# Splitting fp32 weights into two fp32r parts: operations of 512 or of 1024 elements

## The reference

```python
h = rmsnorm(x, norm_mix_g)
q, k, v, glu, gate_a, gate_c = split(h @ w_in)             # 2048 x 9216
attn = stick_breaking(q, k, v)                             # 16 heads x 64
conv = silu(layernorm(depthwise_conv(glu_a * sigmoid(glu_b), 31 taps)))
mixed = sigmoid(gate_a) * (attn @ w_pa) + sigmoid(gate_c) * (conv @ w_pc)
x = x + mixed @ w_out
h = rmsnorm(x, norm_ffn_g)
qry = h @ w_query                                          # 8 heads x 2 x 128
top 16 of 128 x 128 experts per head by product keys; gate = softmax(scores)
x = x + sum over chosen e of gate[e] * gelu(h . expert_u[e]) * expert_v[e]
y = rmsnorm(x, norm_final_g)
```

## The kernel before

| pairs | tiles of | what DVE and ACT do in between |
|---|---|---|
| 0 to 19 | q, k, v, GLU input | norm of the input, products with gathered cache pages |
| 20 to 35 | the gates | four groups of four heads of attention; 240 taps of the convolution |
| 36 to 39 | attention branch | sigmoids of the gates, layer norm, silu |
| 40 to 43 | convolution branch | `t2`, `gates`, `mx` (hi and lo of the mixed tile) |
| 44 to 51 | output projection | residual `x`, `raw2` (hi and lo), squares |
| 52 to 59 | queries | norm, scores by sub-keys |
| 60 to 123 | expert_u (the u stage) | routing (top 16), later one-hot matrices that sum into W |
| then 2 x 128 halves | expert_v, two passes | `whl` (hi and lo of a chunk of W), W times gelu(u), gathered rows for the last 32 tokens (`gacc`) |

## Time and profile before

### The profile page before, as it was taken

How to read it: one execution, slowest core, us unless ns; L and a number is a source line. 1 busy time by engine, 2 the same in 40 slices (tenths; PEclk the granted TensorE clock), 3 DMA queues, 4 the chain that set the end, 5 groups by cost and what they waited for, 6 DMA issues and landing times.

```text
span 2321.4 us, 54702 instructions
## 1 busy us (share of the span) xinstructions
PE 2273.6 (98%) x16868; PEld 2182.1 (94%) x16868; DVE 1778.7 (77%) x3349; ACT 1307.8 (56%) x2485; POOL 281.0 (12%) x339
## 2 busy tenths in 40 slices
PE   8999999999999999999999999999999999999997
PEld 7999889999999999999999999999998888999996
DVE  7775498887766667787878888886788887777777
ACT  6445355557454344444457777775655555555564
POOL 0321100002011000000000000001611112111110
PEclk9999999999999999999999999999999999999998
DMA  6887544435555456666656555556898897777774
GB/s 215 288 289 257 193 138 155 146 129 194 182 181 201 158 166 202 203 203 205 196 184 211 187 184 186 191 189 211 283 295 295 293 304 276 247 254 248 250 259 140
DMA packets 158358, 498.38 MB, mean 215 GB/s; under 512 B 20272, under 2 KB 43192, under 8 KB 158144
## 3 DMA queue, kind: packets, MB, share of 16 engines
q1 hardware_dynamic: 136096, 425.46, 57.3%
q0 software_dynamic: 22176, 71.89, 8.1%
HBM read 472.10 MB, written 25.11 MB: 214 GB/s over the span
## 4 chain that ended last, share of the span: by engine, by line
PE 57%; DMA 3%; DVE 1%; issue 1%; ACT 1%; SPq 0%; DVEq 0%; ACTq 0%
PE ps L2015 16%; PE ps L302 10%; PE ps L305 10%; PE ps L301 10%; PE ps L2019 8%; DMA raw<-expert_v 3%; PE ps L1990 1%; ACT hi L284 0%; DMA gat<-expert_v,gidx 0%; DVE whl L1861 0%; DVE lo L289 0%; PE ps L2033 0%; SPq L1512 0%; DMA raw<-u_tiles 0%; DVE gacc L1867 0%
## 5 line engine op out<-in xcount | busy, mean ns | idle before, releaser
L289 DVE TENSOR_TENSOR lo<-raw,hi 128x512 fp32r<-128x512 f32 x1504 | 1022.7, 694 | 386.3 <-ACT hi L284 333.6
L284 ACT CAST hi<-raw 128x512 fp32r<-128x512 f32 x1504 | 922.1, 618 | 591.7 <-PE ps L305 442.6
L301 PE MATMUL ps<-h_hi,hi 128*128 128x264 f32 (+1 forms) x3200 | 822.6, 286 | 5.0 <-DVE h_lo L878 2.7
L302 PE MATMUL ps<-h_lo,hi 128*128 128x264 f32 (+1 forms) x3200 | 820.0, 286 | 0.0
L301 PEld LDWEIGHTS ps<-h_hi,hi 128*128 128x128 f32 x3200 | 602.7, 188 | 13.7 <-issue 8.6
L302 PEld LDWEIGHTS ps<-h_lo,hi 128*128 128x128 f32 x3200 | 602.7, 188 | 0.1
L2015 PE MATMUL ps<-whl,hi 128*128 128x464 f32 x2048 | 521.0, 376 | 12.8 <-DVE whl L1861 10.7
L305 PE MATMUL ps<-h_hi,lo 128*128 128x264 f32 (+1 forms) x3200 | 523.4, 285 | 3.5 <-DVE lo L289 3.5
L305 PEld LDWEIGHTS ps<-h_hi,lo 128*128 128x128 f32 x3200 | 444.4, 188 | 5.0 <-DVE lo L289 4.9
L2015 PEld LDWEIGHTS ps<-whl,hi 128*128 128x128 f32 x2048 | 349.0, 191 | 41.3 <-issue 17.0
L2019 PEld LDWEIGHTS ps<-whl,lo 128*128 128x128 f32 x2048 | 307.9, 190 | 22.6
(11 more groups left out here) (285 smaller groups left out, 1960.8 us busy)
## 6 DMA issues: line engine op xcount, KB each, us to landing
raw<-u_tiles SPq DMA_DIRECT2D x256, 512.0 KB, 3.7
raw<-expert_v SPq DMA_DIRECT2D x256, 512.0 KB, 5.4
raw<-weights SPq DMA_DIRECT2D x240, 512.0 KB, 3.5
u_spill<-ust POOLq DMA_DIRECT2D x128, 132.0 KB, 2.9
urg<-u_spill SPq DMA_DIRECT2D x32, 464.0 KB, 6.4
qb<-q_spill POOLq DMA_DIRECT2D x8, 512.0 KB, 5.8
x<-xT SPq DMA_DIRECT2D x4, 560.0 KB, 6.8
kvT<-qkv SPq DMA_DIRECT2D x1, 2240.0 KB, 12.5
```

The lines of the kernel that those rows point to most:

```text
L284: nc.scalar.copy(hi[k % SPLIT][:], raw_quarter(k)).then_inc(hi_done, 1)
L289: nc.vector.tensor_tensor(lo[k % SPLIT][:], raw_quarter(k), hi[k % SPLIT][:].bitcast(F32), ALU.subtract).then_inc(lo_done, 1)
L301: pe.matmul(out, a, rhs[0][:, first + j, 0:n], start=start and j == 0, stop=False)
L302: pe.matmul(out, a, rhs[1][:, first + j, 0:n], start=False, stop=False)
```

## The change

One ACT operation and one DVE operation now split both quarters of a half. The buffers are two halves for `hi` and two for `lo`, in the room of the four quarters; `hi[s]` and `lo[s]` become views of them, so that the matmuls read the same addresses. An operation is issued at odd k, for quarters k-1 and k, with the waits that the split of quarter k had; at even k nothing is issued. The semaphores go up by 2. All else stays as it is: PE's waits, the loads, the order and AHEAD. Since AHEAD is 3, the operations stand at the first and the third of the four positions of a tile, and in the passes over expert_v at the first of the two.

```diff
-    hi = [place(f"hi{s}", at["raw"] + 2048 * s, [P, QT, P], F32R) for s in range(SPLIT)]
-    lo = [place(f"lo{s}", at["hi3"] + 2048 * s, [P, QT, P], F32R) for s in range(SPLIT)]
-    ident = place("ident", at["lo3"], [P, P])
+    hi_half = [place(f"hi_half{s}", at["raw"] + 4096 * s, [P, HALF, P], F32R) for s in range(2)]
+    lo_half = [place(f"lo_half{s}", at["hi_half1"] + 4096 * s, [P, HALF, P], F32R) for s in range(2)]
+    hi = [hi_half[s // 2][:, QT * (s % 2):QT * (s % 2) + QT] for s in range(SPLIT)]
+    lo = [lo_half[s // 2][:, QT * (s % 2):QT * (s % 2) + QT] for s in range(SPLIT)]
+    ident = place("ident", at["lo_half1"], [P, P])
...
-    def raw_quarter(k):
-        return raw[:, k // 2 % RAW, QT * (k % 2):QT * (k % 2) + QT]
-
     def split_hi(act, q0, k):
 
-        act.wait_ge(raw_in[k // 2 % RAW], 2 * q0 + 16 * (k // (2 * RAW)) + 16)
-        act.wait_ge(mm_done, q0 + k + 1)
-        nc.scalar.copy(hi[k % SPLIT][:], raw_quarter(k)).then_inc(hi_done, 1)
+        if k % 2:
+            act.wait_ge(raw_in[k // 2 % RAW], 2 * q0 + 16 * (k // (2 * RAW)) + 16)
+            act.wait_ge(mm_done, q0 + k + 1)
+            nc.scalar.copy(hi_half[k // 2 % 2][:], raw[:, k // 2 % RAW]).then_inc(hi_done, 2)
 
     def split_lo(dve, q0, k):
-        dve.wait_ge(hi_done, q0 + k + 2 * RAW + 1)
-        dve.wait_ge(mm_done, q0 + k + 1)
-        nc.vector.tensor_tensor(lo[k % SPLIT][:], raw_quarter(k), hi[k % SPLIT][:].bitcast(F32),
-                                ALU.subtract).then_inc(lo_done, 1)
+        if k % 2:
+            dve.wait_ge(hi_done, q0 + k + 2 * RAW + 1)
+            dve.wait_ge(mm_done, q0 + k + 1)
+            nc.vector.tensor_tensor(lo_half[k // 2 % 2][:], raw[:, k // 2 % RAW], hi_half[k // 2 % 2][:].bitcast(F32),
+                                    ALU.subtract).then_inc(lo_done, 2)
```

## The result

| | before | after |
|---|---|---|
| median of the timed executions | 2317.95 us (4 executions) | 2348.75 us (4 executions, 2348.38 to 2355.24) |
| ratio | | 1.0136, 95% interval 1.0116 to 1.0155 |
| profiled execution, its span | 2322.99, 2321.4 us | 2348.38, 2346.8 us |
| mean granted clock of PE | 0.993 | 0.995 |

The kernel got slower by 31 us; 2339 had been predicted, within 2324 to 2355. The direction and the range held. The size did so partly by luck: one stage, the u stage, cost 12 us more than foreseen, and the passes over expert_v gave back 12 us more.

A forecast was written before the change was run, and what follows sets the result against it. PE (TensorE), busy 98% of the span, was taken to bound the kernel. Terms 8.8+4.3+5.3+2.8+1.4-4.5+0.4 = +18.5 us on 2320.2 gave 2339, range 2324 to 2355.

The forecast's parts named there:

- Steps 1 and 4: Convolution branch tiles (pairs 40 to 43): late hi and lo, +8.8 us; attention branch tiles (pairs 36 to 39): stalls, +2.8.
- Step 3: Gate tiles (pairs 20 to 35): softplus between two pairs delays PE, +1.35 us each, +1.25 in the first group; sum +5.3.
- Step 2: Output projection (pairs 44 to 51, 16 tiles): hi just in time, lo late by 0.27 us a tile; +4.3 us.
- Step 7: Everything else, including start, projection tiles with page products (slack 1.2 us) and routing (slack 1.4): nothing; pass boundary +0.4 us.
- step 5: Start of the u stage, +0.8 us, and ACT's split released by a late transfer at 1222.95, +0.6.
- Step 6: Two passes over expert_v: longer time for transfers to land removes most waits for whl; -4.5 us, bounds -9 and +2.
- the reduction stall: In the passes over expert_v: the forecast said this stall stays.
- A: Faster: stalls after readouts do not appear, savings act in the expert_v passes; 2312 us with 1 us of stalls; chance 0.06.
- B: Near nothing: steps 1 to 4 cost half (10.6 us), expert_v passes give the full 9; +3.4, 2324 us; chance 0.10.
- C: Stalls of 1.1 us in each branch tile halve the granted clock; +47 us for 8 tiles, 2386; chance 0.03.
- D: Raw ring becomes the bound, later releases delay transfers in each group of four halves; +26 us, 2369; chance 0.06.
- E: Change does not do what it says: same number of operations on ACT and DVE; no chance given.

The follow-up runs named there:

- act_half: Changed kernel's order, ACT operations of 1024 elements, each DVE one as two of 512; ratio 1.0041 to the kernel before, 9.7 us more.
- dve_half: Changed kernel's order, ACT with two operations of 512 elements, DVE with one of 1024; ratio 1.0106 to the kernel before, 25 us more.
- square_late: Changed kernel, but in pairs 44 to 51 ACT's square comes behind the following tile's first split; ratio 1.0111 to the kernel before.
- all_two: Changed kernel's order everywhere, each 1024-element operation as two of 512 at the same position; 2310.8 us, ratio 0.9955 to the kernel before.
- v_two: Kernel before, but in the expert_v passes both quarters split at one position, as two operations of 512; 2310.0 us, ratio 0.9944.

## Why the prediction was right or wrong

**Steps 1 and 4 held**: +9.2 and +3.4 against +8.8 and +2.8. Each was a walk along one read-out with the new durations.

**Step 3 held in sum, +4.8 against +5.3, but partly by luck.** In the gates PE now waits 1.08 us per softplus:

```profile
375.05 0.76 PE L306 MATMUL ps<-h_hi,lo_half 128*128 128x264 f32 x4 [1.08 <-DVE lo_half L290]
...
437.58 0.75 PE L306 MATMUL ps<-h_hi,lo_half 128*128 128x264 f32 x4 [1.06 <-DVE lo_half L290]
```

A group of four heads takes 62.53 us here (437.58 - 375.05), 61.51 before: +1.0 rather than the +1.35 of the step, three times. The first group cost more, about 1.7 instead of the 1.25 of the step, and hardly by DVE's lateness: its waits were 2.5 us before (0.26, 1.05 and 1.22) and 2.9 in one piece after. Behind that one PE's clock fell (timeline of PE and the view by stretches, kernel after):

```profile
310.49 1.09 PE L306 MATMUL ps<-h_hi,lo_half 128*128 128x264 f32 x4 [2.88 <-DVE lo_half L290]
313.14 1.08 PE L306 MATMUL ps<-h_hi,lo_half 128*128 128x264 f32 x4
315.03 0.66 PE L306 MATMUL ps<-h_hi,lo_half 128*128 128x264 f32 x4
```
```profile
311.00:314.00 3.00, 3.00 (x15) 3.00 (x15) 3.00 (x7) 0.00 (x0) 0.00 (x0) 0.50 0.52 178
```

Two quarters take 4.54 us instead of 2.92. The other three kernels with merged operations here (`act_half`, `dve_half`, `square_late`) had a wait of 2.5 to 2.9 us at this place and 0.50 behind it too; `all_two`, whose longest wait here was 1.6, kept 1.00, and so did the kernel before.

**Step 2 had the right mechanism and half the size**: 0.48 us a tile, not 0.27. The chain was right (`square_late`); hi and lo together are late by 0.34, 0.07 more than I had, and I had not counted the 0.1 us that PE loses after a wait. At 0.27 a tile such a constant is no detail.

**Step 7 failed at the top-k part**, which it left at nothing because "routing" had 1.4 us of slack. Measured: +12.6 alone, +13.7 with the rest of the stage, against the +1.4 of step 5. The slack was about right. It was set against the interval between two neighbouring splits instead of against the backlog of a whole stretch. The earlier trace rows don't show it either: they were read for single releases.

**Step 7 at the start** was also too kind, by 3 us by the marks and more behind them: the mark at the first Sigmoid is at 175.2 to 178.6 in the four kernels with merged operations there on one engine or both, at 170.1 to 173.3 in the others. From the same matmul to the same, the kernel after loses 5.4 us between 31 and 91; the mark shows only 3.1 because the kernel before had lost some 3 to its clock just ahead. Of the 5.4, over 2 are a wait too short to be listed, once in every two quarters from 36.9 to 62.1 (3.15 us from one group of 0.76 to the next instead of 2.92); timeline of PE, kernel after:

```profile
43.17 0.76 PE L306 MATMUL ps<-h_hi,lo_half 128*128 128x264 f32 x4
44.75 0.65 PE L306 MATMUL ps<-h_hi,lo_half 128*128 128x264 f32 x4
46.32 0.76 PE L306 MATMUL ps<-h_hi,lo_half 128*128 128x264 f32 x4
```

Another place is a wait of DVE for a transfer, with the pair now behind it; timelines of DVE and PE, kernel after:

```profile
88.12 1.23 DVE L949 TENSOR_TENSOR prod<-ring,qb 128x1024 f32<-128x1024 f32 x1 [3.37 <-DMA qb<-q_spill]
89.27 1.22 DVE L290 TENSOR_TENSOR lo_half<-raw,hi_half 128x1024 fp32r<-128x1024 f32 x1
```
```profile
90.54 0.78 PE L306 MATMUL ps<-h_hi,lo_half 128*128 128x280 f32 x4 [1.64 <-DVE lo_half L290]
```

Before, DVE waits there for the same transfer, 3.3 us, and PE shows no gap: the longer lead hid it. The step named "slack 1.2" of the product itself and not the wait ahead of it.

**Step 6 had the right place and a third of the size**: -15.7 in the two passes, or some -12.4 without the clock of the kernel before, not -4.5. I had added up PE's listed waits for whl in pass 0 and taken part of them. The pace of the halves was the thing to read: 2.69 against 2.57 us. I also left out pass 1, which gave 4 to 7 us. What decides is the order, as `v_two` shows; I had described that order and then given it the price of the listed waits. That the reduction stall stays was right (2.02 and 2.00 us).

**The sum**: +18.5 forecast, +25.4 between the spans, +31 between the medians. The stages outside the passes came to +41.1 instead of +22.6, the rest to -15.7 instead of -4.1, so two misses of opposite sign kept the result in the range. Stalls at places that I had called covered had a chance of 0.05; they came, and only the passes hid them. Of the rivals, A and B needed the stalls of steps 1 to 4 to be small, which they were not. (A's 2312 leaves out the +1.4 and +0.4 that B counts; with them it is 2314.) C did not come in the branch tiles: the granted clock was 1.00 from 590 to 647, through stalls of 0.7 us a tile. It came once in the gates, behind the wait of 2.88 us, and cost about 1.5 us. D is refuted by ACT's 3.5 us for expert_v; E by x752.

## What to carry to other kernels

When an operation that feeds the bounding engine is made larger, its lead shrinks twice: it can start no earlier, and its first part is ready only at its end. Hold the new lead against the backlog that the feeding engine builds up over its busiest stretch and against every wait ahead of it on its queue, not against its mean load. Before merging, try the move alone: here the moved order alone made the kernel 10 us faster, and merging what was moved 42 us slower. And measure losses by the distance of equal instructions, since listed waits showed little more than half of them here; look at the granted clock on the way, since it alone moved such distances by 3 us between two executions.

## What the runs showed of the hardware

- A wait of PE costs about 0.10 us beyond its length: the group after it is shown as 0.75 long instead of 0.65, and the next group comes 1.56 or 1.57 after it instead of 1.46. It was the same behind a wait of 0.87 us and behind one too short to be listed.
- "Busy" hid idleness: 195.1 of 200 us busy with 1197 matmuls, against 200.0 with 1248 of the same kinds.
- The granted clock can fall behind the same wait in one execution and not in another: 0.50 behind 2.02 us of waiting at 1954.40 in the kernel before, 1.00 behind 2.00 us at 1986.93 in the kernel after. The same 16 matmuls took 3.56 and 1.97 us.
- On two of the three chips the transfers nearly stood still for 20 to 40 us at the start of the passes, in all six profiles taken there. By its times (2357.5 and 2359.8 against 2321.3 us) the kernel before lost as much there, though it was not profiled on these chips. This is `act_half`, view by stretches; the last two columns are the DMA share and GB/s:

```profile
1655.00:1695.00 40.00, 5.79 (x24) 4.93 (x22) 2.09 (x4) 2.45 (x4) 25.59 (x27) 0.60 0.25 74
1700.00:1740.00 40.00, 40.00 (x249) 37.30 (x249) 29.31 (x51) 20.88 (x32) 0.00 (x0) 0.99 0.75 230
```

  In 25 of the 40 us from 1655 on they moved at most 8 GB/s. The granted clock averaged 0.60 over the stretch in which PE was idle for 34 us, and 0.99 in the next. Why the transfers stop on these chips and not on the first stays open.
